# Gates of 64 dense tokens written to a zeroed DRAM matrix by indirect accumulating transfers

## What is computed

```python
s = einsum('nhpd,pkd->nhpk', q, subkeys)           # 8 heads, 2 sides, 128 keys a side
sv, si = top_k(s, 16)                              # best 16 of each side
cand = sv[:,:,0,:,None] + sv[:,:,1,None,:]         # 16 x 16 pairs
cs, ci = top_k(cand, 16)                           # 16 experts (i, j) a head
gate = softmax(cs)                                 # 8 x 16 = 128 gates a token
hid  = gelu(x . u[expert]);  out = sum(gate * hid * v[expert])
```

## Time and profile before

| what | value |
|---|---|
| median of 3 runs | 1794.88 us (1794.35 to 1795.64) |
| span of the profiled execution | 1793.2 us |
| PE busy | 1774.3 us (99%) |
| DVE busy | 1388.5 us (77%) |
| ACT busy | 766.7 us (43%) |
| POOL busy | 170.8 us (10%) |
| moved by DMA | 531 MB, 296 GB/s mean |

### The profile page before, as it was taken

The page is one execution under the profiler, slowest core; times in us unless marked ns, Lnnn a source line. Parts: engine busy times, 40 slices in busy tenths (PEclk is TensorE's granted clock), DMA queues, the critical chain, the costliest instruction groups (busy, mean ns, idle before and its releaser), DMA issues.

```text
span 1793.2 us, 27943 instructions
## 1 busy us (share of the span) xinstructions
PE 1774.3 (99%) x10680; PEld 1591.7 (89%) x10680; DVE 1388.5 (77%) x2153; ACT 766.7 (43%) x1054; POOL 170.8 (10%) x158
## 2 busy tenths in 40 slices
PE   8999999999999999999999999999999999999998
PEld 8899989789999999999977777789999998777775
DVE  6546667566459796888378898989999998898996
ACT  5334444655331010111155555555555555555555
POOL 0000000000000121222100000111111111111010
PEclk9999999999999999999999999999999999999999
DMA  9774544556545987998999899999999999999984
GB/s 351 262 280 149 165 141 142 188 187 226 187 150 192 358 333 282 342 336 331 362 377 361 317 324 341 344 350 367 377 369 374 377 347 361 353 359 365 357 309 152
DMA packets 77275, 531.01 MB, mean 296 GB/s; under 512 B 8811, under 2 KB 9211, under 8 KB 16268
## 3 DMA queue, kind: packets, MB, share of 16 engines
q1 hardware_dynamic: 54512, 377.96, 56.6%
q0 software_dynamic: 22352, 151.59, 23.2%
q10 hardware_dynamic: 332, 0.44, 0.1%
HBM read 512.60 MB, written 15.20 MB: 294 GB/s over the span
## 4 chain that ended last, share of the span: by engine, by line
PE 97%; DVE 1%; issue 1%; ACT 1%; DMA 0%; DVEq 0%; SPq 0%; ACTq 0%
PE bank L918 19%; PE bank L934 11%; PE bank L596 8%; PE bank L597 8%; PE bank L598 8%; PE bank L1015 6%; PE bank L1014 6%; PE bank L1019 6%; PE bank L1021 6%; PE bank L1020 6%; PE bank L935 5%; PE bank L973 2%; PE bank L743 0%; PE bank L952 0%; PE bank L791 0%
## 5 line engine op out<-in xcount | busy, mean ns | idle before, releaser
L1932 DVE TENSOR_TENSOR lo<-raw,hi 128x1024 fp32r<-128x1024 f32 x384 | 463.6, 1221 | 101.7 <-ACT hi L1318 101.3
L1318 ACT ACTIVATE hi<-raw 128x1024 fp32r<-128x1024 f32 x384 | 404.9, 1059 | 320.8 <-PE bank L1021 233.5
L918 PE MATMUL bank<-hT,raw 128*128 128x192 f32 x2048 | 337.4, 326 | 0.0
L918 PEld LDWEIGHTS bank<-hT,raw 128*128 128x128 f32 x2048 | 332.3, 190 | 0.1
L934 PE MATMUL bank<-xr,hi 128*128 128x384 f32 x1024 | 291.3, 359 | 0.0
L935 PE MATMUL bank<-xr,lo 128*128 128x192 f32 x1024 | 256.3, 250 | 0.0
L1444 DVE TENSOR_TENSOR lo<-raw,hi 128x2048 fp32r<-128x2048 f32 x75 | 171.8, 2290 | 103.7 <-ACT hi L1086 68.2
L1015 PE MATMUL bank<-lo,wm 128*64 128x512 f32 x512 | 202.8, 396 | 0.0
L1014 PE MATMUL bank<-hi,wm 128*128 128x512 f32 x512 | 199.9, 390 | 1.7 <-DVE wm L1987 1.2
L1019 PE MATMUL bank<-lo,wm 128*128 128x512 f32 x512 | 200.3, 391 | 0.0
L1021 PE MATMUL bank<-hi,wm 128*128 128x512 f32 x512 | 199.3, 389 | 0.0
(11 more groups left out here) (293 smaller groups left out, 2686.2 us busy)
## 6 DMA issues: line engine op xcount, KB each, us to landing
raw<-in_u SPq DMA_DIRECT2D x128, 1024.0 KB, 7.7
raw<-in_v SPq DMA_DIRECT2D x128, 1024.0 KB, 7.2
raw<-in_w_in SPq DMA_DIRECT2D x43, 1024.0 KB, 5.8
raw<-in_w_out SPq DMA_DIRECT2D x16, 1024.0 KB, 4.8
raw<-in_wq SPq DMA_DIRECT2D x16, 1024.0 KB, 4.8
gate_matrix<-gs POOLq DMA_DIRECT2D x12, 768.0 KB, 12.5
gs<-gate_matrix SPq DMA_DIRECT2D x12, 768.0 KB, 9.2
raw<-in_cmp_w SPq DMA_DIRECT2D x8, 1024.0 KB, 4.8
```

What stands on the lines that cost most here:

```text
L918: last = mm(bank[s % 2][:, 0:TD], raw[:, s, k * P:(k + 1) * P], xn[:, k, 0:TD], start=(k == 0), stop=(k == KT - 1))
L1318: do(hi[:, s % 2, cols], raw[:, s, cols], ACT.Copy).then_inc(v_hi_ready, 1)
L1932: vec.tensor_tensor(lo[:, n % 2, cols], raw[:, n % RAW, cols], hi[:, n % 2, cols].bitcast(F32), ALU.subtract).then_inc(v_lo_ready, 1)
```

## The change

The one-hot products are made for tokens 0 to 127 alone (16 batches instead of 24, `MATRIX_T = range(0, P)`), and only the first tile's choices are transposed. The gates of tokens 128 to 191 go to `gate_matrix` by another way, and the matrix now has all 16 groups of 8 blocks:

- POOL clears the matrix by 8 DMAs (1536 KB each) from a zeroed tile, four after weight blocks 12, 16, 20 and 24, four after 28, 32, 36 and 40.
- DVE computes for each chosen slot of the second tile the number of its cell in the matrix (`find_cells(1)`), between the two `route_tokens`.
- POOL moves numbers and gates of 64 tokens to a tile of 128 x 64 by four small DMAs, and then issues 64 indirect DMAs (`add_gate`), each of which adds 128 gates (64 tokens, two slots each) to their cells. Two stand at each b from 14 to 45, ahead of the gathers of that b. Ahead of every eighth, POOL waits until all earlier ones have landed. The gathers of b = 14 come behind the moves.
- `apply_gates` treats tokens 0 to 127 alone. In v blocks 0 to 31 DVE multiplies the gates of tokens 128 to 191 (64 columns) from loaded groups.
- SP loads the first two groups of gates behind v loads 0 to 3, after waits for adds and stores. There are 16 gate loads instead of 12, and 8 stores instead of 12. `round_gated(0, 0)` moves behind the last u block, to wait for `gated`.
- In the first half of the u blocks ACT's gelus of the sparse items come 5 blocks later (`GELU_LAG`).

```diff
-GATE_BLOCKS, BATCHES = HALF - ROUTED, TD // 8
+MATRIX_T = range(0, P)
+GATE_BLOCKS, BATCHES = HALF - ROUTED, len(MATRIX_T) // 8
+ADDED = SLOTS // 2
+ADD_WINDOWS = {1: (14, 46)}
+ZERO_PARTS, ZERO_W = 8, 2 * TD
+GELU_LAG = 5
...
-        gate_dram = nc.dram_tensor("gate_matrix", (STORED_GROUPS, P, TD, GROUP_J), F32, kind="Internal").ap()
+        gate_dram = nc.dram_tensor("gate_matrix", (GROUPS_J, P, TD, GROUP_J), F32, kind="Internal").ap()
...
+                if half == 0:
+                    for r in range(RAW):
+                        load_v(r, r)
+                    sp.wait_ge(gates_added, 16 * ADDED * 1)
+                    for x in range(2):
+                        sp.wait_ge(gate_stored[x], 16 * (BATCHES // 4))
+                    for g in range(2):
+                        load_gates(g, g)
...
+            def clear(c):
+                pool.wait_ge(block_done, PAIRS + 4 * (c + 1))
+                n = TD * NKEYS // ZERO_PARTS
+                pool.dma_start(gate_parts[:, c * n:(c + 1) * n].rearrange("p (a w) -> p a w", w=ZERO_W),
+                               zeros.unsqueeze(1).to_broadcast([P, n // ZERO_W, ZERO_W])).then_inc(gate_zeroed, 16)
...
+            def move_cells(tt):
+                gates = choice[:, 2, tt]
+                pool.wait_ge(choices_listed, {1: 2, 0: 3}[tt])
+                for src, dst in ((cells[:, tt, :], cell_at), (gates, cell_gate)):
+                    by_head = src.rearrange("p (h x k) -> p x h k", h=PH, x=2)
+                    for x in range(2):
+                        pool.dma_start(dst[TS * x:TS * (x + 1), tt, :].rearrange("p (h k) -> p h k", h=PH),
+                                       by_head[0:TS, x]).then_inc(choices_moved, 16)
+            move_cells(1)
...
+            def add_gate(tt, n):
+                h, k = n // (PK // 2), n % (PK // 2)
+                if n == 0:
+                    pool.wait_ge(choices_moved, {1: 96, 0: 160}[tt])
+                    pool.wait_ge(gate_zeroed, 16 * ZERO_PARTS)
+                elif k == 0:
+                    pool.wait_ge(gates_added, 16 * (n + {1: 0, 0: ADDED}[tt]))
+                pool.indirect_dma_start(gate_cells, bass.IndirectOffsetOnAxis(ap=cell_at[:, tt, n:n + 1], axis=0),
+                                        cell_gate[:, tt, n:n + 1], None, compute_op=ALU.add).then_inc(gates_added, 16)
...
+                for tt in (1,):
+                    for n in range(added_by(tt, b - 1), added_by(tt, b)):
+                        add_gate(tt, n)
                 ahead = range(items_by(b - 1), items_by(b))
...
             route_tokens(1, 0)
             dv.wait_ge(choices_ready, 1)
+            find_cells(1)
...
+                    x = mv + HALF * half
+                    g, r = x // GROUP_J % 2, x % GROUP_J
+                    if r == 0:
+                        dv.wait_ge(gate_loaded[g], 16 * (x // (2 * GROUP_J) + 1))
+                    if x >= 2:
+                        dv.wait_ge(wm_lo, x - 1)
+                    dv.wait_ge(acc_evacuated, M_PEER + HALF * half + min(mv + 2, HALF))
+                    gates_of = gs[:, g, 0:TD * GROUP_J].rearrange("p (t j) -> p t j", j=GROUP_J)[:, :, r]
+                    if half == 0 and mv < GATED_EARLY:
+                        rest = gated_rows.rearrange("p (a t) -> p a t", t=TS)[:, 2:3, :]
+                        gates_of = gates_of.rearrange("p (a t) -> p a t", t=TS)[:, 2:3, :]
+                        vec.tensor_tensor(rest, rest, gates_of, ALU.mult).then_inc(gated, 1)
```

More of the change, by code:

```diff
@@ L96, in items_by, with added_by @@
     return sum(n * min(max(b + 1 - first, 0), last - first) // (last - first) for first, last, n in STAGE_ITEMS)
+def added_by(tt, b):
+    first, last = ADD_WINDOWS.get(tt, (0, 0))
+    return ADDED * min(max(b + 1 - first, 0), last - first) // (last - first) if last else 0
 def buffer_of(i):
@@ L112, in gelus_at, with seen @@
 def gelus_at(b):
-    return [q for q in range(PAIR_TILES // GROUP) if items_by(b - 1) >= group_end(q) > items_by(b - 2)]
+    def seen(b):
+        return items_by(b - 1 - (GELU_LAG if b < HALF else 0))
+    return [q for q in range(PAIR_TILES // GROUP) if seen(b) >= group_end(q) > seen(b - 1)]
 def group_end(q):
@@ L495, in _ @@
                         sp.dma_start(h_first, res_dram[:, 0:1024]).then_inc(gf_loaded, 16)
-                    x = first + q - early
+                    x = HALF // GROUP_J * half + q
                     if x >= 2:
@@ L533, in _ @@
                 pool.dma_start(bias[:, :, P * part:P * part + P * (part + 1)], skew).then_inc(bias_loaded, 16)
+            pool.wait_ge(consts_ready, 2)
+            def clear(c):
[3 more added lines that the diff above has]
+                               zeros.unsqueeze(1).to_broadcast([P, n // ZERO_W, ZERO_W])).then_inc(gate_zeroed, 16)
+            for c in range(ZERO_PARTS // 2):
+                clear(c)
             pool.wait_ge(acc_evacuated, RK + 4)
@@ L539, in _ @@
                                ).then_inc(halves_swapped, 16)
+            for c in range(ZERO_PARTS // 2, ZERO_PARTS):
+                clear(c)
             pool.wait_ge(acc_evacuated, M_WQ)
@@ L960, in _ @@
             pe.wait_ge(q_copied, 8)
-            for x in range(6):
-                last = nc.tensor.transpose(bank[2 + x // 4][:, (x % 4) * P:(x % 4 + 1) * P], choice[:, x // 2, x % 2, :], ident)
+            for x in range(3):
+                last = nc.tensor.transpose(bank[2][:, x * P:(x + 1) * P], choice[:, x, 0, :], ident)
             last.then_inc(ch_turned, 1)
@@ L1344, in round_gated @@
                 weights = hidden[:, mv * TD:(mv + 1) * TD]
+                ac.wait_ge(gated, mv + (HALF * half + 1))
                 if half or mv >= GATED_EARLY:
[L1346 removed]
                     weights = wmt[:, (mv % 2) * TD:(mv % 2 + 1) * TD]
@@ L1385, in _ @@
                         round_split(2 * HALF * half + mv)
-                        if half and mv < 2:
-                            hidden_gelu(HALF - 2 + mv)
-                        round_gated(half, mv)
+                    if half and mv < 2:
+                        hidden_gelu(HALF - 2 + mv)
+                    round_gated(half, mv)
                     pair_gelus((2 * half + 1) * HALF + mv)
@@ L1459, in _ @@
             vec.memset(eps, EPS).then_inc(consts_ready, 1)
+            vec.memset(zeros, 0.0).then_inc(consts_ready, 1)
             dv.wait_ge(first_hi, 1)
@@ L1832, in _, with find_cells @@
             ci4 = ci.rearrange("p (t h k) -> p t h k", t=2, h=PH)
+            def find_cells(tt):
+                f, u = cells_f, cells[:, tt, :]
+                step(vec.tensor_copy(u, choice[:, 1, tt]))
+                routed()
+                step(vec.tensor_scalar(u, u, GROUP_J - 1, None, ALU.bitwise_and))
+                routed()
+                step(vec.tensor_copy(f, u))
+                routed()
+                step(vec.scalar_tensor_tensor(out=f, in0=f, scalar=float(1 - P * TD), in1=token_at[:, tt:tt + 1].to_broadcast([P, SLOTS]),
+                                              op0=ALU.mult, op1=ALU.add))
+                routed()
+                step(vec.scalar_tensor_tensor(out=f, in0=choice[:, 0, tt], scalar=float(TD * GROUP_J), in1=f, op0=ALU.mult, op1=ALU.add))
+                routed()
+                step(vec.scalar_tensor_tensor(out=f, in0=choice[:, 1, tt], scalar=float(P * TD), in1=f, op0=ALU.mult, op1=ALU.add))
+                routed()
+                vec.tensor_copy(u, f).then_inc(choices_listed, 1)
             def route_tokens(tt, items):
```

75 lines of the change are left out of this document (36 added, 39 removed).

## The result

| | before | after |
|---|---|---|
| median | 1794.88 us | 1836.86 us (4 runs, 1831.55 to 1840.42) |
| ratio, 95% interval | | 1.0233 [1.0215, 1.0250] |
| span of the profiled execution | 1793.2 us | 1838.6 us |
| PE busy | 1774.3 us | 1770.6 us |
| POOL busy | 170.8 us | 314.0 us |

The account below looks back on a forecast made before the run. The prediction took PE's own stream as the bound. Its terms, -14.6 + 5.8 + 13.2 + 4.0 + 0.1, with 0.2 for clears and lesser gaps, gave +8.7: span 1801.9, median 1803.6 us, range 1796 to 1819.

Parts of the forecast that it names:

- Removed, -14.6: Between u blocks: 8 of 24 gate batches (14.3 us) and three of six transposes (0.3) leave PE's chain.
- Clears, 0: Weight blocks from 12 on: the eight clears of 1536 KB cost PE nothing.
- The other end of the forecast, 4.4: Upper bound for the clears: +4.4 us if one clear's transfer time falls wholly on PE once.
- The routing, 5.8 at block 32: PE waits 5.8 us at block 32's transposes: routing ends 8.7 us later, less 2.87 of slack; bounds 4 and 10.
- I take nothing for them: The other 34 adds before block 32 fit POOL's idle time of 4.28 to 8.13 us before gathers: 0.
- All 8.7 pass to its chain: In the routing, the first gather leaves 8.7 us later and DVE's chain is delayed by all of it.
- find_cells as costed: On DVE between the routing of the two tiles: 7 instructions, 1.9 us with their gaps.
- My first rival: Adds cost POOL 2.24 us each and overfill gaps between gathers; routing shifts 20 to 25 us, 1815 to 1820; chance 0.12.
- The second rival: Adds hold the ring that gathers use, 2.4 us each; routing ends 40 to 50 us later, about 1845; chance 0.06.
- The first gate load, 13.2: v block 0 starts 13.2 us later, waiting for gates loaded behind four v loads; between 10.9 and 15.9.
- The clock, 4.0: PE's clock falls after the waits at block 32 and v block 0: 2.0 us lost each, 4.0 together.
- The v blocks, 0.1: v blocks: 32 small products join DVE, 7 to 9 us, adding 0.1 us to PE's waits.

Follow-up runs that it names:

- e4: The kernel before with 16 gate batches instead of 24 and nothing added, gates of tokens 128 to 191 left out: 1793.6 us, ratio 1.0001.
- e5: The kernel before with 16 gate batches, nothing added, and ACT's gelus of sparse items 5 blocks later in the first half: 1795.4 us, ratio 1.0001.
- e10: The changed kernel without find_cells, moves and adds, clears after blocks 20 to 48, first gate loads between v loads 1 and 2: 1790.2 us.
- e3: The changed kernel with the eight clears after weight blocks 20 to 48 instead of 12 to 40: 1830.7 us.
- e1: The changed kernel with the 64 adds at b = 32 to 55 instead of 14 to 45: 1825.6 us.
- e7: The changed kernel with the 64 indirect transfers as plain writes, without the addition: 1820.9 us.
- e2: The changed kernel with the first two gate loads issued ahead of v loads 0 to 3 instead of behind them: 1826.6 us.

## Why the forecast was wrong, step by step

**Removed, -14.6: true of PE's own work, wrong as a gain by itself.** I read the earlier trace rows as "PE never idle" and stopped there; the DMA share in the same row, 0.84 over 373 us, hides 0.55 for the first 62 us and 0.91 over 700 to 900, with 1.01 in its last 20. Fewer batches leave the loads less time for the same bytes. Alone they gave 0 (e4, e5), with the change's fewer stores 4.8 us of the median (e10). In the changed kernel the 14.6 us did leave the stretch, and waits of 21.3 us and a lower clock stand in it; how many of these the removal brought about, no run separates.

**Clears, 0: 2.7 us.** The first clear meets the blocks that load two tiles at once (e3). The other end of the forecast, 4.4, held it.

**The routing, 5.8 at block 32: 25.6. This is the step that failed.** "I take nothing for them", the 34 adds behind the first two, was wrong. POOL's gaps of 4.3 to 8.1 us were compared with two adds of 1.25 each, a size taken from a gather (0.94 and a gap). An add took 1.57 in the median (1.54 at best) and 2.01 in the mean, with 0.30 to the next, and a wait for landed adds comes ahead of every eighth. The 36 adds of the routing held POOL for 71.6 us, some 83 with their gaps, and the routing ended 31.6 us later after u block 0 than before (202.4 against 170.8), where the forecast had 8.7. Of the 71.6 us about 34 are a gather's price, 23 the addition's own (0.63 each) and 15 DVE's products beside them (estimates from 0.94, 1.57 and the durations in this trace).

"All 8.7 pass to its chain" failed too. The first gather left 14.8 us later (604.65 - 518.70, against 587.16 - 515.98), made of 2.5 more for the pairs, 2.7 and 3.7 for the moves and their wait, 3.9 for two adds, and find_cells as costed. But e1 has 7.5 of these and ends its routing 0.8 late: the gaps win a late head back, as long as nothing fills them.

My first rival had this mechanism, adds that no longer fit the gaps, and nearly this price, 2.24 each. It had 20 to 25 us of shift and laid the price to DVE's products alone; it lost its chance because slow issues were taken for the exception. Of the 36 adds 13 were slow in that way, and the rest still cost 1.57. The second rival, a held ring, is not what happened: the rows landed no later than before (e7), and POOL waited for landed adds for 11.8 us in all.

**The first gate load, 13.2: 14.6.** Right in place, cause and size; e2 took it away and put a late v load in its place.

**The clock, 4.0: 10.6.** PE's busy time shows it: 3.4 us more in the routing, 5.5 in the next stretch and 1.7 behind v block 0, for the same products less the batches. PE worked for 18.8 us at half clock in this trace, which accounts for 9.4 of the 10.6. The changed kernel behind the two long waits, granted clock third from the end:

```profile
721.20:737.30 16.10, 16.10 (x89) 16.10 (x90) 6.74 (x20) 1.17 (x5) 5.58 (x4) 0.83 0.29 83
...
944.80:960.00 15.20, 15.20 (x59) 11.61 (x60) 9.71 (x15) 6.01 (x8) 0.00 (x0) 0.87 0.64 216
```

More waits than two, and longer ones, so more stretches at half clock (1.2 GHz instead of 2.4).

**The v blocks, 0.1: 1.5**, nearly all of it clock (PE busy 883.6 against 881.9 us).

**What the sum did not have:** 1.6 us for a u load, and 5.1 us of waits in the batches (2.1 for DVE's one-hots, 3.0 without a releaser in the trace).

With these the trace closes: -14.6 + 2.7 + 25.6 + 14.6 + 10.6 + 1.6 + 5.1 = +45.6, against 45.4 of span. Of the 36.7 us by which the forecast span was short, 19.8 are the wait at block 32 and 6.6 the clock behind the waits.

## What to carry to other kernels

A gap on the engine that issues transfers is not free room until the new transfers are priced with their own duration, their spacing and their waits, and summed over the stretch: once the gap is used up, more work is passed on to whoever needs the transfers queued behind. Taking work from the busiest engine pays only as far as the next bound lets it: read the DMA share slice by slice in the stretch that gets shorter, for its bytes stay. An experiment that does only the removal is the first to run.

## What the runs showed of the hardware

- **An indirect transfer with an addition costs POOL 1.57 us in the median, without it 0.98**, for the same 128 pieces of 4 bytes, and makes 112 packets more. The bytes are the same: it is a price on the issuing engine.
- **An issue that meets a long DVE product ends a fixed time after the product.** The adds at 612.87 and 618.14 began 0.6 and 0.2 us after DVE's rows of 128x2048 at 612.26 and 617.93, shown above, and ended at 615.98 and 621.64: 1.43 and 1.42 us after those rows ended (614.55 and 620.22). All 23 adds over 1.8 us in the changed kernel end 1.42 to 1.50 us after a DVE instruction with two inputs in SBUF (SCALAR_TENSOR_TENSOR or TENSOR_TENSOR), the plain writes of e7 0.83 to 0.88 us after one, so the add waits for the product and then takes nearly its whole time. A TENSOR_REDUCE of 128x2048, with one input, held up none: the add at 694.04, beside the one from 692.35 to 694.63, took 1.54. The Trainium skill ("SBUF — State Buffer", SBUF: two separate sides) describes an exclusive lock on the port pair that DVE and GpSimd share, which a DVE instruction with two SBUF inputs takes only against a GpSimd one that reads SBUF; the trace agrees, for adds as for the gather of 2.44 us in the earlier trace rows, which ends 0.81 us after such a product.
- **A load's landing depends on what the queues hold:** 21.2 us for a v load of 1 MB behind two gate loads in e2, where 7.2 is the median of the kernel before.
